# Row scalings of the attended rows and of the delta rule's output moved from VectorE to ScalarE and GpSimd, and a weight copy moved within ScalarE's step

## The reference

```python
sb_o = stick_breaking_attention(...)             # 4 heads x 64
sb_o = rms_norm(sb_o, sb_gain)
dn_o = gated_delta_rule(...)                     # 4 heads x 128
dn_o = rms_norm(dn_o, dn_gain) * jax.nn.silu(split_heads(dn_z, DN_HEADS))
hg_o = hgrn2_recurrence(...)                     # 4 heads x 64
hg_o = rms_norm(hg_o, hg_gain) * jax.nn.sigmoid(split_heads(hg_g, HG_HEADS))
mix = jnp.concatenate([sb_o, dn_o, hg_o], axis=-1)
x = x + mix @ w_out                              # then a SwiGLU FFN and a last norm
```

## Time and profile before

| | us |
|---|---|
| median of 3 runs | 1379.13 |
| lowest, highest | 1377.3, 1385.66 |
| the profiled execution, its own time | 1385.77 |
| its span in the profile | 1384.0 |
| TensorE busy, share of the span | 1333.4, 96% |
| VectorE busy | 783.5, 57% |
| ScalarE busy | 592.7, 43% |
| GpSimd busy | 674.3, 49% |
| granted TensorE clock, mean | 0.983 |

### The profile page before, as it was taken

How to read it: one execution, slowest core, us unless ns; L and a number is a source line. 1 busy time by engine, 2 the same in 40 slices (tenths; PEclk the granted TensorE clock), 3 DMA queues, 4 the chain that set the end, 5 groups by cost and what they waited for, 6 DMA issues and landing times.

```text
span 1384.0 us, 24260 instructions
## 1 busy us (share of the span) xinstructions
PE 1333.4 (96%) x9101; PEld 1106.9 (80%) x9101; DVE 783.5 (57%) x1171; ACT 592.7 (43%) x1403; POOL 674.3 (49%) x583
## 2 busy tenths in 40 slices
PE   5999999999999998888999999999999999999997
PEld 4777887978888777767888788888888888788886
DVE  5014635557354488984147965655555556665657
ACT  6234535445343466662133433333333334344445
POOL 3224324133253477760300876676666677754442
PEclk9999999999999799998999999999999999999999
DMA  5131322323225342514210244554555545876653
GB/s 184 33 105 51 97 62 87 119 73 118 66 78 137 103 128 83 188 57 157 61 31 1 84 151 149 157 160 149 171 175 155 164 145 206 310 267 197 190 191 122
DMA packets 160371, 178.60 MB, mean 129 GB/s; under 512 B 9520, under 2 KB 110464, under 8 KB 160256
## 3 DMA queue, kind: packets, MB, share of 16 engines
q1 hardware_dynamic: 160112, 176.53, 39.9%
q10 hardware_dynamic: 144, 0.52, 0.1%
HBM read 124.32 MB, written 52.71 MB: 128 GB/s over the span
## 4 chain that ended last, share of the span: by engine, by line
PE 86%; DVE 5%; issue 3%; POOL 2%; ACT 1%; DMA 1%; SPq 0%; DVEq 0%; ACTq 0%; POOLq 0%
PE banks L2416 9%; PE banks L2418 9%; PE banks L2417 9%; PE banks L353 6%; PE banks L355 6%; PE banks L354 6%; PE banks L2427 4%; PE banks L2428 4%; PE banks L2429 4%; PE banks L692 2%; PE banks L693 2%; PE banks L694 2%; PE banks L2108 2%; PE banks L2110 2%; PE banks L2109 2%
## 5 line engine op out<-in xcount | busy, mean ns | idle before, releaser
L2574 POOL TENSOR_TENSOR w_l<-area,w_h 128x512 fp32r<-128x512 f32 x119 | 175.4, 1479 | 180.2 <-ACT w_h L2469 135.0
L2574 POOL TENSOR_TENSOR w_l<-w_raw,w_h 128x512 fp32r<-128x512 f32 x100 | 140.4, 1405 | 99.8 <-ACT w_h L2524 50.3
L353 PE MATMUL banks<-act_h,w_h 128*128 128x512 f32 x352 | 141.4, 402 | 0.0
L355 PE MATMUL banks<-act_h,w_l 128*128 128x512 f32 x352 | 137.6, 391 | 0.0
L354 PE MATMUL banks<-act_l,w_h 128*128 128x512 f32 x352 | 137.2, 390 | 0.0
L341 POOL TENSOR_TENSOR w_l<-w_raw,w_h 128x1024 fp32r<-128x1024 f32 x24 | 59.4, 2478 | 142.5 <-ACT w_h L334 125.3
L2416 PE MATMUL banks<-act_h,w_h 128*128 128x512 f32 x320 | 124.5, 389 | 0.0
L2417 PE MATMUL banks<-act_l,w_h 128*128 128x512 f32 x320 | 124.5, 389 | 0.0
L2418 PE MATMUL banks<-act_h,w_l 128*128 128x512 f32 x320 | 124.5, 389 | 0.0
L2427 PE MATMUL banks<-w_h,act_h 128*128 128x512 f32 x308 | 120.1, 390 | 0.4 <-DVE act_l L2726 0.4
L2428 PE MATMUL banks<-w_l,act_h 128*128 128x512 f32 x308 | 119.8, 389 | 0.0
(11 more groups left out here) (316 smaller groups left out, 3347.2 us busy)
## 6 DMA issues: line engine op xcount, KB each, us to landing
w_raw<-in_w_in SPq DMA_DIRECT2D x22, 512.0 KB, 3.9
w_raw<-in_w_gate SPq DMA_DIRECT2D x22, 512.0 KB, 4.5
area<-in_w_up SPq DMA_DIRECT2D x22, 512.0 KB, 4.6
ff_wide<-in_w_down SPq DMA_DIRECT2D x22, 512.0 KB, 4.2
down_sums<-ff_wide SPq DMA_DIRECT2D x11, 1024.0 KB, 4.1
area<-in_x SPq DMA_DIRECT2D x8, 1024.0 KB, 7.9
projected_tm<-area SPq DMA_DIRECT2D x32, 256.0 KB, 2.4
hidden_sums<-area SPq DMA_DIRECT2D x6, 1024.0 KB, 4.2
```

The costliest lines, as they stand in the source:

```text
L353: e.matmul(dst, w_h[:, b, k], act_h[:, k, cols], start=(k == 0), stop=False)
L355: mm = e.matmul(dst, w_l[:, b, k], act_h[:, k, cols], start=False, stop=(k == KT - 1))
L2574: e.tensor_tensor(slot(w_l, u), raw_use(u) if u < NU_FF else wd_raw(u - NU_FF), slot(w_h, u).bitcast(F32), ALU.subtract).then_inc(sems["fl ...
```

## The change

`final_sb` and `final_dn` were products on VectorE, in one instruction for each head: source times the head's length scale (a number for each row) times gain or gate. Each is cut in two. ScalarE copies the source with the row's scale into `mix` (`attended_scaled` in two pairs of heads, `delta_scaled` in four instructions from PSUM); GpSimd then multiplies `mix` in place by gain (`final_sb`, one 128x256 instruction) or gate (`final_dn`, one of 128x512). `final_hg` stays on VectorE. TensorE's waits for bank 5 to be read are now for `dn_scaled`, and `m_turn` has a new one. ScalarE's `out_high(0, t)` stands after `inverse(u, 1)` and no longer at the step's end.

```diff
@@ PE: turn, query_state, m_turn
                 if lv == 0:
-                    reach(e, "fin_dn", c - 1)
+                    reach(e, "dn_scaled", c - 1)
...
                 reach(e, "s_new", c)
-                reach(e, "fin_dn", c)
+                reach(e, "dn_scaled", c)
...
             def m_turn(c):
                 e.wait_ge(sems["m"], c + 1)
+                reach(e, "dn_scaled", c - 1)
@@ ACT
             def lengths(c):
                 e.wait_ge(sems["dn_sq"], c + 1)
-                reach(e, "fin_dn", c)
...
+            def delta_scaled(c):
+                e.wait_ge(sems["dn_r"], 2 * c + 2)
+                reach(e, "mt_done", 2 * c)
+                for h in range(DNH):
+                    ins = e.activation(mix[:, SBW + h * P:SBW + (h + 1) * P], bank(5)[:, h * P:(h + 1) * P], ACT.Copy, scale=r_dn[:, h:h + 1])
+                ins.then_inc(sems["dn_scaled"], 1)
+
+            def attended_scaled(c, first):
+                e.wait_ge(sems["pb_loaded"], 16 * (c + 1))
+                e.wait_ge(sems["pre_act"], 5)
+                reach(e, "mt_done", 2 * c - 1)
+                for h in (first, first + 1):
+                    cols = slice(SB_AT - 2 * DNW + h * SBD, SB_AT - 2 * DNW + (h + 1) * SBD)
+                    ins = e.activation(mix[:, h * SBD:(h + 1) * SBD], pb[:, cols], ACT.Copy, scale=r_sb[:, c, h:h + 1])
+                ins.then_inc(sems["sb_scaled"], 1)
@@ ACT step
                 if live(u):
                     inverse(u, 1)
+                if 0 <= t < 4:
+                    out_high(e, 0, t)
...
                     to_end(u)
+                if live(t):
+                    attended_scaled(t, 0)
                 if live(u):
                     inverse(u, 3)
+                if live(t):
+                    attended_scaled(t, 2)
...
                     whole_inverse(u)
-                if 0 <= t < 4:
-                    out_high(e, 0, t)
+                if live(t):
+                    delta_scaled(t)
@@ DVE step
                 if live(t):
-                    final_sb(t)
                     take(t, 4)
...
                     queries(u, 3)
-                if live(t):
-                    final_dn(t)
@@ POOL
+            def final_sb(c):
+                e.wait_ge(sems["sb_scaled"], 2 * c + 2)
+                tt(mix[:, 0:SBW], mix[:, 0:SBW], gain_row[:, 0:SBW], ALU.mult, "fin_sb")
+
+            def final_dn(c):
+                e.wait_ge(sems["dn_scaled"], c + 1)
+                e.wait_ge(sems["gated"], c + 1)
+                tt(mix[:, SBW:SBW + DNW], mix[:, SBW:SBW + DNW], gate[:, 0:DNW], ALU.mult, "fin_dn")
@@ POOL step
                         spread(u, lv)
+                if live(t):
+                    final_sb(t)
                 if live(u, NT - 1):
                     decayed_keys(u)
...
                     values(u)
+                if live(t):
+                    final_dn(t)
                 if 0 <= t < 4:
                     out_low(e, 0, t)
```

More of the change, by code:

```diff
@@ L284, in trunk_program @@
                 f_ln hg_sq hg_r t_copied kdt vn act_high eb kde h_el dn_sq dn_r egr span
-                r xy tt hs_new f_log h_b h_sc e_cut act_low s_new h_qe h_fs m at0 fin_dn fin_hg fin_sb
+                r xy tt hs_new f_log h_b h_sc e_cut act_low s_new h_qe h_fs m at0 sb_scaled dn_scaled fin_dn fin_hg fin_sb
                 qd at vb gated h_dl t_init qb h_bk kd
@@ L1828, in scores @@
                 tt(at[:, c % 2], heads(bank(3)), span[:, :, :], ALU.mult, "at0")
[L1830 to L1841, removed]
             def final_hg(c):
@@ L1846, in final_hg @@
                 reach(e, "mt_done", 2 * c)
[L1847 to L1853, removed]
+                for h in range(4):
+                    cols = slice(h * HGD, (h + 1) * HGD)
+                    at = SBW + DNW + h * HGD
+                    ins = e.scalar_tensor_tensor(out=mix[:, at:at + HGD], in0=bank(7)[:, cols], scalar=r_hg[:, h:h + 1],
+                                                 in1=gate[:, DNW + h * HGD:DNW + (h + 1) * HGD], op0=ALU.mult, op1=ALU.mult)
+                ins.then_inc(sems["fin_hg"], 1)
             def step(t):
```

## The result

The changed kernel took 1390.27 us (median of 6 runs, 1389.13 to 1395.27), the kernel before beside it 1379.57 (6 runs, 1377.3 to 1385.66): a ratio of 1.0063, 95% interval 1.0041 to 1.0086. It is slower, by 8.7 us by that ratio and 10.7 by the medians, where 1376.5 was forecast and 1385 was the upper end. The profiled execution took 1395.27 us (span 1393.3); it is the slowest of the six, 5 us above their median.

What follows compares the result with a forecast made beforehand. No engine was full; work passed back and forth, with VectorE's two-SBUF-input rows waiting for GpSimd's running instruction. Terms +1.5 + 1.8 - 3.1 - 2.6 - 0.2 = -2.6 us took 1379.1 to 1376.5 us, range 1367 to 1385.

Steps and rivals of the forecast that it cites:

- the sum: Whole kernel: the gains and losses of all places added, +1.5 + 1.8 - 3.1 - 2.6 - 0.2 = -2.6 us.
- rival 2: Steps with out_low: the new delay halves the clock, up to 7 us per fall; chance 0.14 for one, 0.06 for more.
- if the clock row shows a half between 490 and 615: A sign in the new profile, named beforehand, that the forecast is wrong: half clock between those times.
- Ends of steps 1 to 3: final_dn on GpSimd delays out_low and so residual: net +0.75 us in steps 1 and 3, +1.4 in step 2.
- At the end of step 0 ... 0: End of step 0: ScalarE and TensorE are late anyway, so the delay of out_low costs 0.
- Ends and scans: Step ends sum to +1.5 us; the scans behind them, pushed into by causal, unit and key_logs, to +1.8.
- final_sb off VectorE: Steps 1 to 5: queries(u, 1) waits for GpSimd, queries(u, 2) comes earlier, take(t, 7) starts 0.7 us earlier, except step 2.
- final_dn off VectorE: Behind take(t, 7): frees 1.11 us of VectorE, but TensorE's chain ends last there, so 0 by itself.
- Step 6: Takes start earlier, -3.1 us; TensorE's gap goes and the clock stays, -2.6.
- Rivals 1 and 3: 1: VectorE's time returns, about 1359, chance 0.04; partly, 1370, 0.22. 3: step 6 gains less, 1379 to 1380.5, 0.14.
- Prices: Moved work, each step: ScalarE's four scalings 1.26 us, GpSimd's 128x512 product 1.27 and its 128x256 product about 0.8.
- Tail: Steps 7 and 8: takes need scores that end 0.2 us before they start, so only -0.2 of 0.87.

Runs made afterwards that it cites:

- e7: The changed kernel with GpSimd's final_dn behind out_low instead of ahead of it; 1383.5 us, ratio 1.0006.
- e8: The changed kernel with 6 dummy TensorE products ahead of update(u, 1) in steps 1 to 6; 1377.07 us, ratio 0.9966.
- e2: The changed kernel with GpSimd's out_low moved from the step's end to between final_sb and decayed_keys; 1373.23 us, ratio 0.9934.
- e9: The changed kernel with final_dn back on VectorE and out_low between final_sb and decayed_keys on GpSimd; 1371.1 us, ratio 0.9922.
- e3: The kernel before with only final_sb moved to ScalarE and GpSimd; final_dn and out_high as before; 1380.31 us, ratio 0.9975.
- e6: The changed kernel with final_sb back on VectorE, out_high still in mid-step; 1393.88 us, ratio 1.0073.
- e10: The changed kernel with ScalarE's delta_scaled ahead of its decays; 1386.37 us, ratio 1.002.
- e5: The kernel before with out_high behind inverse(u, 1) on ScalarE and out_low ahead of decayed_keys on GpSimd; 1403.32 us, ratio 1.0151.
- e4: The kernel before with a dummy GpSimd product of 1.27 us ahead of out_low in steps 0 to 3; 1390.66 us, ratio 1.0072.

## Why the prediction was wrong

**The step that failed** is the clock in steps 1 to 5, for which the sum has no term: the new TensorE gaps were priced as waiting alone. What they do to the clock stood only as rival 2, "The new delay halves the clock in the steps with `out_low`", held at 0.14 for one fall and 0.06 for more, and "if the clock row shows a half between 490 and 615" is what happened: 41 us at 1.2 GHz, which cost 13. The forecast had worked out both gaps (1.8 and 1.1; measured 1.66 to 1.71 and 1.08 at the starts of steps 2 to 4, 2.01 and 0.80 at that of step 1) and had a fall behind one of 1.90 in its own rows. It took falls for rare accidents, each less likely than the last. But the work from step to step is the same, so the gaps repeat, and falls come in most steps that have them: in all four here, behind three of the four gaps of 2.6 us in e7. One fall alone was the unlikely case. Its price was off too: up to 7 us for each of three, against 2 to 4 in each of steps 1 to 5 (changed kernel less e8: 1.96, 3.86, 3.81, 3.81, and 1.91 in step 5, of which 1.54 is the gap without a cause shown).

**The sum without it was right.** e8 is the changed kernel without half clock in steps 1 to 5. Lengths in us, from the windows and starts:

| | before | changed | e8 | e2 |
|---|---|---|---|---|
| step 0 | 29.61 | 23.78 | 23.86 | 22.62 |
| steps 1 to 5 | 112.81 | 131.31 | 115.96 | 110.06 |
| step 6 | 25.02 | 19.07 | 19.52 | 19.05 |
| from 7 on | 753.71 | 756.43 | 753.82 | 752.83 |

From step 1 on e8 is 2.2 us below before; the sum had -2.6. That is from one execution of each, and e8 has its dummies to pay (0.45 us in step 6).

- Ends of steps 1 to 3: by its terms 7.7 to 7.8 us from last take to `residual`, measured 7.53 to 7.54; `log_sigmoids` ends 0.28 after out_low, said 0.3. "At the end of step 0 ... 0" was a miss: 7.96 in e8 against 7.28 in e9. The 8.61 before, on which that rested, belonged to a step at half clock.
- Ends and scans: +3.3 forecast for steps 1 to 5, +3.15 in e8. The scans take 1.74, and TensorE's second gap of 1.08 stands at the starts of steps 2 to 4, as said.
- final_sb off VectorE: `queries(u, 1)` 0.72 (said 0.8) and `queries(u, 2)` 0.32 (0.35) in step 6, and in e8's steps 1 to 5 0.70 to 0.72 and 0.33 to 0.34. In the changed kernel's steps 1 to 5, at half clock, they meet other products and take 0.28 and 0.69 to 0.70. The takes are earlier: e2's steps 4 and 5 are 1.36 and 0.70 shorter than before, said 0.7.
- final_dn off VectorE, "0 by itself": e9 against e2 bears it out.
- Step 6: -3.1 and -2.6 forecast, -5.95 measured; e3 and e6 show it to be final_sb's alone. Rivals 1 and 3 fell with this and with the delay.
- Prices: scalings 1.14 (1.26), GpSimd's products 1.28 (1.27) and 0.73 (0.8). Right to 0.12.
- Tail: -0.2 forecast, +2.7 in the changed kernel. There a TensorE gap of 3.36 us, at the place where 2.24 stood before, goes with 6.8 us at half clock from 659.6 on. In e8, at +0.1, that gap is 2.56 and 3.4 us at half clock follow; in e2, at -0.9, it is 2.52 and none do. Why it is longer in the changed kernel isn't shown: TensorE waits for nothing that the profile shows.

**On the clock** steps 2 to 4 are at 0.81 each. The Trainium skill, "TensorE: Matmul & The Clock Gate", section "HAM oscillation — how this bites in real kernels", tells of a kernel that loses the clock again in every tile, because each brings the same wait. The trace agrees in kind, and this repetition is what the forecast missed. The gaps that the page names are longer than those here, so by their length alone it would have spoken for the forecast.

**On the lock** the Trainium skill, "SBUF — State Buffer", section "SBUF: two separate sides", is borne out: the waiting row is held to the end of the whole instruction. The forecast used it for single rows; e7, e10 and e5 show what it does to a row of them: one VectorE row for each GpSimd product, 5.29 us for four rows of 0.28.

## What to carry to other kernels

A delay that returns with each step of a loop, and leaves TensorE idle where it wasn't, is priced twice: once with the clock kept, and once with a fall in most of the steps, since falls repeat with the gap. A few dummy products in the gap tell in one experiment which it is. One profile doesn't: the mean clock of every run belongs beside it, as e3, e4 and e6 show. Before work goes to GpSimd, write down what VectorE runs at that moment: rows with two SBUF inputs pass one for each GpSimd product, rows from PSUM pass freely. An idle stretch of GpSimd beside such rows isn't free room, while one beside PSUM reads is; and of a change with several parts, the part without the gain can carry the loss.

## What the runs showed of the hardware

- Added work made the kernel faster: 1.60 us of dummy products in a gap of 1.7 saved 13 us, since the clock stayed at 2.4 GHz for 41 us more of steps 1 to 5.
- In the changed kernel the falls of steps 2 to 4 came after a gap of 1.7 us and one of 1.1, that of step 1 after one of 2.0; in e4 and e6 the first came after one of 2.2, and more came in steps with gaps of 0.4 and 0.9 to 1.0; e3 with 0.4 and 1.1 had none in its profile.
- VectorE's rows with two SBUF inputs and GpSimd's products take turns one for one: four rows of 0.28 us in 5.29 (e7) and 5.30 (e10), four of `final_sb` in 3.63 instead of 0.87 (e5).
- The same gap of 1.90 us in step 0 was followed by 23.9 us at half clock in one profiled execution (before), by 3.4 in others (changed, e2) and by none in e6 and e9. The runs of the kernel before alone range from 0.980 to 0.996 in mean clock, so a difference of this kind lies at least in part between executions.
